# A hybrid decoder step on one core: state sums one unit sooner, two output strips interleaved, and a new order of the last steps

## The chip, the cores and the metric

One core of a Trainium2 chip runs one launch of the kernel. The metric is the device time in microseconds (us), as the median of the runs.

## The reference

One step of a hybrid decoder layer, for a prompt of 256 tokens (with 16 learned meta tokens ahead of it) and for 8 samples of one token. D is 2048, there are 8 heads with DK = 128 and DV = 256, and the feed-forward width is 5632.

```python
h = rmsnorm(x, norm1_g)
z = h @ w_in                              # u, cg, bg, q, k, v, o, gates, g_a, g_b
a_out = bg * causal_dwconv(cg * u)
hb    = mlstm_sequence(q, k, v, ...)      # per head: C = carry * C + sum g k v^T
mix   = sigmoid(g_a) * a_out + sigmoid(g_b) * sigmoid(o) * hb
x     = x + mix @ w_out
up    = causal_dwconv(rmsnorm(x, norm2_g) @ w_up)
x     = x + (silu(up[..., D_FF:]) * up[..., :D_FF]) @ w_down
y     = rmsnorm(x, norm_f_g)              # written for the prompt and the samples
```

The matrix memories C, the normalisers n and m, and the rows of both convolutions are outputs as well. All tensors are float32.

## The kernel before

Everything lives on one core, with the 280 tokens along the free dimension and features along the partitions. All four large products use the same **unit**: 8 tiles of 128 by 128 of the weight matrix (1024 columns of a slot), one column block of 128 outputs. Each unit passes four engines in turn. SP loads it into `w_raw` (512 KB), ScalarE (ACT) copies it into `w_hi`, which rounds it to the type fp32r, VectorE (DVE) writes the rest into `w_lo = w_raw - w_hi`, and TensorE (PE) multiplies: per tile `w_hi` with the high and the low part of the activations (16 matmuls, L1324), then `w_lo` with the high part (8 matmuls, L1329). There are 4 slots (`RING`), so the semaphores let ACT write `w_hi` of unit u+4 only when PE has used unit u (`unit_used`), and let SP load again into a slot when DVE has written its `w_lo` (`lo_done`). Two units make a **strip**, whose sum gathers in one PSUM bank (strip0 to strip3 in turn) and is then taken out by DVE. `evacuated` counts strips taken out, and the second half of a strip waits for the bank of the next one.

The program has these stages, each engine with its own list of instructions written out by hand:

- The start: loads, transposes of x, the first norm (`rtok`, spread over partitions as `rbc`) and the gates.
- Eight heads. Each has 16 strips of `w_in`, which are units 0 to 31 of the head. Functions `front` (units 0 to 7) and `back` (units 8 to 31) of each engine hold the order: the loop variable `i` is the unit's number in the head, `step(n, HEAD_U, 0, i)` splits the unit that is 4 later (i + 4), and the work of the head is inserted between the steps. In `back`, GpSimd (POOL) updates the sample states `c_st` in four pairs (L564, L565, L569, semaphore `c_updated`). DVE sums each pair with the query into `sacc` (L1056, L1060), in the steps i = 16, 17, 18 and 19, adds both halves (L1065) in i = 19, and PE multiplies them with `sel` (L1436) after strip 10, which is unit 21. That is the **state sum**. In the same steps DVE takes out the strips `ga` (i = 15), `go` (17) and `gb` (19) on L889, and ACT has its sigmoids of them in the same list as the copies to `w_hi`.
- The output projection: 16 strips of `w_out`, the activations are `mh` and `ml`, in 16 tiles. The last tile comes from the last head: POOL makes `mx`, DVE splits it into `mh` and `ml` (L1097, L1100, semaphore `mix_split`, 2 for each tile). Then a norm over the new x (`refine` on `rbc`).
- The feed-forward part in two halves: strips of `w_up`, the gated unit, strips of `w_down` (3 units each).
- The end: in the last 16 down strips, DVE adds x (L1199) and scales by the gain (L1204), PE transposes the result back to tokens (`turn_y`, L1227), ACT squares (L786) and POOL adds the squares into `acc` (L612). After the last strip PE sums `acc` over partitions (L1528, one column for each token tile), DVE, ACT and DVE again make 1/sqrt of the mean (L1208, L858, `refine`), and the rows are scaled: ACT the second 128 tokens in four column blocks, each followed by its own store (L866, L868), DVE the first 128 tokens in four blocks and the samples (L1218, L1220, L1221), which SP stores (L423, L425).

`refine` is a Newton step for 1/sqrt and is called three times: at the start on 128x3, after the output projection on 128x266, and at the end on 128x3. Two places carry the order of the state sum and of the end:

```python
if 16 <= i < 20:                                   # DVE, back(n)
    jp = i - 16
    v.wait_ge(c_updated, n * (JG // 2) + (jp + 1))
...
turn_y(KT - 1)                                     # PE, the end
pe.wait_ge(acc_done, 2 * KT + 1)
```

## Time and profile before

| what | value |
|---|---|
| median of 3 runs | 1744.8 us |
| lowest and highest | 1744.09 and 1752.38 us |
| the profiled execution, its own time | 1743.8 us |
| its span, first to last instruction | 1742.0 us |
| granted TensorE clock, mean | 0.997 |
| PE busy | 1721.4 us (99%) |
| DVE, ACT, POOL busy | 1157.7, 743.4, 482.7 us |

Busy time of PE is modelled: the matmuls overlap, and the end of each is an estimate, so its stalls are best read from the starts of two successive instructions. The time of the execution is 1.8 us above the span.

### The profile page before, as it was taken

What the parts mean: (1) busy time and instruction counts of PE and PEld (TensorE: products, weight loads), DVE (VectorE), ACT (ScalarE), POOL (GpSimd) and SP (SyncE); (2) the same over time, 40 slices, a digit from 0 to 9 for tenths busy, and PEclk for the clock granted to TensorE, in tenths of its full rate; (3) what the DMA queues carried; (4) which work ended last, traced back from release to release, by engine and by line L of the source; (5) the groups of instructions that cost most, each with busy time, mean ns of one, the idle gap of its engine ahead of it and who ended that gap; (6) DMA issues with size and microseconds to landing.
All of it is one profiled execution on the core that took longest, in us unless ns stands there. A gap on an engine that the chain in (4) does not pass through costs nothing.

```text
span 1742.0 us, 37212 instructions
## 1 busy us (share of the span) xinstructions
PE 1721.4 (99%) x13797; PEld 1706.3 (98%) x13797; DVE 1157.7 (66%) x1776; ACT 743.4 (43%) x867; POOL 482.7 (28%) x474
## 2 busy tenths in 40 slices
PE   9999999999999999999999999999999999999997
PEld 7999999999999999999999999999999999999997
DVE  4774757657485765748677887777555777777553
ACT  6534334344433433443345554554343333334443
POOL 3541615234161523416211222222000222222000
PEclk9999999999999999999999999999999999999998
DMA  7878685777868678786665666666666666666663
GB/s 192 205 198 194 181 212 149 214 189 203 199 176 206 159 212 186 201 207 172 183 172 159 188 186 174 179 177 176 183 179 186 171 180 180 176 179 181 172 178 105
DMA packets 591287, 318.78 MB, mean 183 GB/s; under 512 B 16695, under 2 KB 585847, under 8 KB 589103
## 3 DMA queue, kind: packets, MB, share of 16 engines
q1 hardware_dynamic: 578855, 293.13, 62.5%
q10 hardware_dynamic: 11944, 22.14, 4.6%
q0 software_dynamic: 400, 2.20, 0.5%
q8 instruction: 72, 1.18, 0.3%
q14 instruction: 16, 0.13, 0.0%
HBM read 305.07 MB, written 12.78 MB: 182 GB/s over the span
## 4 chain that ended last, share of the span: by engine, by line
PE 91%; DVE 5%; issue 3%; ACT 1%; DMA 0%; POOL 0%; DVEq 0%; ACTq 0%; SPq 0%; POOLq 0%
PE strip L1324 57%; PE strip L1329 29%; DVE w_lo L880 2%; PE aux L1227 1%; DVE sacc L1060 1%; PE aux L1420 1%; PE aux L1424 1%; DVE rden L1041 1%; DVE sacc L1056 0%; ACT w_hi L620 0%; PE aux L1393 0%; PE aux L1277 0%; PE strip L1260 0%; DMA x_tok<-in_x_prompt 0%; PE aux L1436 0%
## 5 line engine op out<-in xcount | busy, mean ns | idle before, releaser
L880 DVE TENSOR_TENSOR w_lo<-w_raw,w_hi 128x1024 fp32r<-128x1024 f32 x556 | 718.2, 1294 | 380.0 <-ACT w_hi L620 377.7
L620 ACT ACTIVATE w_hi<-w_raw 128x1024 fp32r<-128x1024 f32 x560 | 593.4, 1060 | 869.0 <-PE strip L1329 841.0
L1324 PE MATMUL strip<-xh,w_hi 128*128 128x266 f32 (+2 forms) x3424 | 866.4, 287 | 0.0
L1324 PE MATMUL strip<-xl,w_hi 128*128 128x266 f32 (+2 forms) x3424 | 864.5, 286 | 0.0
L1324 PEld LDWEIGHTS strip<-xh,w_hi 128*128 128x128 f32 x3424 | 644.8, 188 | 0.3
L1324 PEld LDWEIGHTS strip<-xl,w_hi 128*128 128x128 f32 x3424 | 644.1, 188 | 0.0
L1329 PE MATMUL strip<-xh,w_lo 128*128 128x266 f32 (+2 forms) x3424 | 494.1, 286 | 0.0
L1329 PEld LDWEIGHTS strip<-xh,w_lo 128*128 128x128 f32 x3424 | 451.4, 188 | 0.0
L1324 PE MATMUL strip<-hh,w_hi 128*128 128x264 f32 x704 | 176.2, 286 | 0.0
L1324 PE MATMUL strip<-hl,w_hi 128*128 128x264 f32 x704 | 174.7, 283 | 0.0
L604 POOL TENSOR_TENSOR gg<-sg,cz 128x264 f32<-128x264 f32 x44 | 58.2, 1322 | 412.1 <-ACT sg L825 412.1
L1324 PEld LDWEIGHTS strip<-hh,w_hi 128*128 128x128 f32 x704 | 132.4, 188 | 0.3
L1324 PEld LDWEIGHTS strip<-hl,w_hi 128*128 128x128 f32 x704 | 132.3, 188 | 0.0
L607 POOL TENSOR_TENSOR hid<-gg,cz 128x264 f32<-128x264 f32 x44 | 73.5, 1671 | 104.7 <-DVE cz L1168 104.7
L1329 PE MATMUL strip<-hh,w_lo 128*128 128x264 f32 x704 | 100.6, 283 | 0.0
L1329 PEld LDWEIGHTS strip<-hh,w_lo 128*128 128x128 f32 x704 | 91.5, 188 | 0.0
L1324 PE MATMUL strip<-mh,w_hi 128*128 128x266 f32 x256 | 64.5, 286 | 0.9 <-DVE ml L1100 0.9
L1324 PE MATMUL strip<-ml,w_hi 128*128 128x266 f32 x256 | 64.4, 286 | 0.0
L889 DVE TENSOR_TENSOR zs<-strip,rbc 128x266 f32<-128x266 f32 x88 | 37.9, 431 | 25.2 <-PE strip L1329 25.2
L578 POOL TENSOR_TENSOR so<-so,sbm 128x266 f32<-128x266 f32 x16 | 20.6, 1287 | 117.3 <-ACT sbm L765 117.3
L1160 DVE SCALAR_TENSOR_TENSOR cz<-zs,vecs,cz 128x256 f32<-128x256 f32 x88 | 42.7, 485 | 12.9 <-DVE cz L1157 2.1
L569 POOL TENSOR_TENSOR c_st<-c_st,kv 128x512 f32<-128x512 f32 x32 | 50.4, 1575 | 2.5
(284 smaller groups left out, 1262.5 us busy)
## 6 DMA issues: line engine op xcount, KB each, us to landing
w_raw<-in_w_in SPq DMA_DIRECT2D x256, 512.0 KB, 4.3
w_raw<-in_w_up SPq DMA_DIRECT2D x176, 512.0 KB, 4.1
w_raw<-in_w_down SPq DMA_DIRECT2D x64, 512.0 KB, 3.9
w_raw<-in_w_out SPq DMA_DIRECT2D x32, 512.0 KB, 4.0
w_raw<-in_w_down SPq DMA_DIRECT2D x32, 384.0 KB, 3.3
out<-c_st ACTq DMA_DIRECT2D x8, 1024.0 KB, 7.1
c_st<-in_state_mlstm_C ACTq DMA_DIRECT2D x7, 1024.0 KB, 11.2
rb<-scratch_rows ACTq DMA_DIRECT2D x8, 270.0 KB, 4.6
```

What stands on the lines that cost most here:

```text
L569: g.tensor_tensor(c_p, c_p, kv[:, :, :], ALU.add).then_inc(c_updated, 1)
L578: g.tensor_tensor(so[:, :], so[:, :], sbm[:, :], ALU.mult).then_inc(p_gate, 1)
L604: g.tensor_tensor(gg[:, :], sg[:, :], cz[:, 0, :], ALU.mult).then_inc(gg_done, 1)
L607: g.tensor_tensor(hid[:, :], gg[:, :], cz[:, 1, :], ALU.mult).then_inc(hid_done, 1)
L620: act.activation(w_hi[:, slot, :], w_raw[:, slot, :], ACT.Copy).then_inc(hi_done, 1)
L880: v.tensor_tensor(w_lo[:, slot, :], w_raw[:, slot, :], w_hi[:, slot, :].bitcast(f32), ALU.subtract).then_inc(lo_done, 1)
L889: v.tensor_tensor(out, bank[b][:, 0:width], rbc[:, c0:c0 + width], ALU.mult).then_inc(evacuated, 1)
L1041: v.reciprocal(rden[:, :], den[:, :])\
L1060: v.scalar_tensor_tensor(out=sacc[:, a, :], in0=c_st[:, jg, :], scalar=qkd_g[:, jg:jg + 1], in1=sacc[:, a, :], op0=ALU.mult, op1=ALU.add). ...
L1160: v.scalar_tensor_tensor(out=cz[:, z, 0:SEQ], in0=zs[:, z, 1:1 + SEQ], scalar=wcol[1], in1=cz[:, z, 0:SEQ], op0=ALU.mult, op1=ALU.add)\
L1324: pe.matmul(bank[b][:, 0:c1 - c0], w_hi[:, slot, w], xt[:, k0 + k, c0:c1], start=(first and k == 0 and t == 0), stop=False)
L1329: mm = pe.matmul(bank[b][:, 0:c1 - c0], w_lo[:, slot, w], rh[:, k0 + k, c0:c1], start=False, stop=(last and k == kk - 1))
```

## The change

Four edits:

- **State sums.** DVE does the four pairs in steps i = 15 to 18 instead of 16 to 19, and the final addition in step 18. The operations are the same.
- **First two output strips.** PE's order was first half and second half of strip 0, then of strip 1. It is now first half of strip 0, first half of strip 1, second half of strip 0, second half of strip 1. The first half of strip 1 does not count as a used unit when it ends (`frees=0`); the second half of strip 0 counts for both.
- **`refine`.** Its last two operations, an addition of 1.5 and a multiplication, become one.
- **The end.** POOL no longer adds the last square. PE sums `acc` with the first 15 squares and then the last square `sqs` itself, into one column each of three PSUM banks, ahead of the last `turn_y`. DVE has three operations for the mean instead of two. Of ACT's four blocks the third (columns 1024 to 1535) goes to DVE and its store to SP. Only the last blocks still wait for the last `turn_y`.

```diff
@@ -417,11 +417,11 @@

-            for h in range(4):
+            for i, (t, h) in enumerate(((0, 0), (0, 1), (0, 2), (1, 2), (0, 3))):
                 c = slice(h * D // 4, (h + 1) * D // 4)
-                sp.wait_ge(y_done, h + 1)
-                sp.dma_start(y_prompt[0, 0:P, c], yt[:, 0, c]).then_inc(stored, 16)
-            sp.wait_ge(y_done, 5)
+                sp.wait_ge(y_done, i + 1)
+                sp.dma_start(y_prompt[0, t * P:(t + 1) * P, c], yt[:, t, c]).then_inc(stored, 16)
+            sp.wait_ge(y_done, 6)
             sp.dma_start(y_sample[:, 0, :], ys[:, :]).then_inc(stored, 16)
@@ -606,7 +606,7 @@
             g.wait_ge(acc_clear, 1)
-            with g.Fori(KT, 2 * KT) as m:
+            with g.Fori(KT, 2 * KT - 1) as m:
                 g.wait_ge(sq_done, m + 2)
@@ -854,17 +854,18 @@
                     act.activation(ys[:, 512 * gq:512 * gq + 512], aux[2][0:NS, :], ACT.Copy).then_inc(y_copied, 1)
-            act.wait_ge(rf_step, 2)
+            act.wait_ge(rf_step, 3)
             act.activation(rfr[:, :], rfm[:, :], ACT.Sqrt).then_inc(rf_root, 1)
...
             act.wait_ge(y_copied, 3 * (KT // 4 - 1))
-            act.wait_ge(y_turned, KT)
-            for h in range(4):
+            for i, h in enumerate((0, 1, 3)):
                 c = slice(h * D // 4, (h + 1) * D // 4)
+                if h == 3:
+                    act.wait_ge(y_turned, KT)
                 src = yt[:, 1, c] if h < 3 else aux[1][:, :]
                 act.activation(yt[:, 1, c], src, ACT.Copy, scale=rf[:, 1:2]).then_inc(y1_done, 1)
-                act.wait_ge(y1_done, h + 1)
+                act.wait_ge(y1_done, i + 1)
                 act.dma_start(y_prompt[0, P:2 * P, c], yt[:, 1, c]).then_inc(stored, 16)
@@ -897,9 +898,8 @@
                 v.wait_ge(done, d0 + 3)
-                v.tensor_scalar(root[0:r, c], root[0:r, c], 1.5, None, ALU.add).then_inc(done, 1)
-                v.wait_ge(done, d0 + 4)
-                v.tensor_tensor(out[0:r, c], out[0:r, c], root[0:r, c], ALU.mult).then_inc(done, 1)
+                v.scalar_tensor_tensor(out=out[0:r, c], in0=root[0:r, c], scalar=1.5, in1=out[0:r, c],
+                                       op0=ALU.add, op1=ALU.mult).then_inc(done, 1)

@@ -928,7 +928,7 @@
             refine(P, slice(0, 3), rms, msq, rtok, rtok_done, 0)
-            v.wait_ge(rtok_done, 5)
+            v.wait_ge(rtok_done, 4)
             for j in range(3):
@@ -1045,9 +1045,9 @@
                          .then_inc(h_step, 1)
-                    if 16 <= i < 20:
-
-                        jp = i - 16
+                    if 15 <= i < 19:
+
+                        jp = i - 15
                         sa0 = n * (JG + 1)
@@ -1060,7 +1060,7 @@
                                                        op0=ALU.mult, op1=ALU.add).then_inc(sacc_step, 1)
-                        if i == 19:
+                        if i == 18:
                             v.wait_ge(sacc_step, sa0 + JG)
@@ -1136,7 +1136,7 @@
             refine(P, slice(0, NM), rt2, rm2, rbc, r2_step, 1)
-            v.wait_ge(r2_step, 6)
+            v.wait_ge(r2_step, 5)

@@ -1205,20 +1205,21 @@
             v.wait_ge(acc_clear, 2)
-            v.tensor_scalar(rfm[:, 0:2], aux[3][:, 0:2], 1.0 / D, EPS, ALU.mult, ALU.add).then_inc(rf_step, 1)
-            v.tensor_scalar(rfm[0:NS, 2:3], aux[3][0:NS, 2:3], 1.0 / D, EPS, ALU.mult, ALU.add).then_inc(rf_step, 1)
+            for j, b in enumerate((aux[3], bank[0], bank[1])):
+                r = P if j < 2 else NS
+                v.tensor_scalar(rfm[0:r, j:j + 1], b[0:r, 0:1], 1.0 / D, EPS, ALU.mult, ALU.add).then_inc(rf_step, 1)
             v.wait_ge(rf_root, 1)
-            refine(P, slice(0, 3), rfr, rfm, rf, rf_step, 2)
+            refine(P, slice(0, 3), rfr, rfm, rf, rf_step, 3)
             v.wait_ge(rf_step, 7)
             v.wait_ge(y_copied, 3 * (KT // 4 - 1))
+            q = D // 4
+            for t, h in ((0, 0), (0, 1), (0, 2), (1, 2)):
+                c = slice(h * q, (h + 1) * q)
+                v.tensor_scalar(yt[:, t, c], yt[:, t, c], rf[:, t:t + 1], None, ALU.mult).then_inc(y_done, 1)
             v.wait_ge(y_turned, KT)
-            for h in range(4):
-                c = slice(h * D // 4, (h + 1) * D // 4)
-                src = yt[:, 0, c] if h < 3 else aux[0][:, :]
-                v.tensor_scalar(yt[:, 0, c], src, rf[:, 0:1], None, ALU.mult).then_inc(y_done, 1)
-            c = 3 * D // 4
-            v.tensor_scalar(ys[:, 0:c], ys[:, 0:c], rf[0:NS, 2:3], None, ALU.mult)
-            v.tensor_scalar(ys[:, c:D], aux[2][0:NS, :], rf[0:NS, 2:3], None, ALU.mult).then_inc(y_done, 1)
+            v.tensor_scalar(yt[:, 0, 3 * q:D], aux[0][:, :], rf[:, 0:1], None, ALU.mult).then_inc(y_done, 1)
+            v.tensor_scalar(ys[:, 0:3 * q], ys[:, 0:3 * q], rf[0:NS, 2:3], None, ALU.mult)
+            v.tensor_scalar(ys[:, 3 * q:D], aux[2][0:NS, :], rf[0:NS, 2:3], None, ALU.mult).then_inc(y_done, 1)

@@ -1311,7 +1312,7 @@

-            def unit(u, slot, b, k0, kk, rh, rl, c0, c1, first, last, waits=()):
+            def unit(u, slot, b, k0, kk, rh, rl, c0, c1, first, last, waits=(), frees=1):

@@ -1328,7 +1329,8 @@
                                    start=False, stop=(last and k == kk - 1))
-                mm.then_inc(unit_used, 1)
+                if frees:
+                    mm.then_inc(unit_used, frees)

@@ -1448,8 +1450,14 @@

-            out_strip(0, 0, tiles_ready(mix_split, 2, 0, KT))
-            for q in range(1, 4):
+            def out_unit(q, h, waits, frees):
+                unit(U_B + 2 * q + h, 2 * q + h, q, h * KU, KU, mh, ml, 0, NM, h == 0, h == 1, waits, frees)
+
+            out_unit(0, 0, ((0, mix_split, KT),), 1)
+            out_unit(1, 0, ((0, evacuated, S_B + 2),), 0)
+            out_unit(0, 1, ((0, mix_split, 2 * (KT - 2)), (KU - 2, mix_split, 2 * (KT - 1)), (KU - 1, mix_split, 2 * KT)), 2)
+            out_unit(1, 1, ((2, evacuated, S_B + 3),), 1)
+            for q in range(2, 4):
                 out_strip(0, q)
@@ -1521,12 +1529,18 @@
                     turn_y(m - 1)
+
+            def sums(squares, first, last):
+                for j, b in enumerate((aux[3], bank[0], bank[1])):
+                    r = P if j < 2 else NS
+                    mm = pe.matmul(b[0:r, 0:1], squares[:, j * P:j * P + r], ones[:, 0:1], start=first, stop=last)
+                return mm
+
+            pe.wait_ge(acc_done, 2 * KT)
+            sums(acc, True, False)
+            pe.wait_ge(sq_done, 2 * KT + 1)
+            sums(sqs, False, True).then_inc(ssqf_done, 1)
             turn_y(KT - 1)
-            pe.wait_ge(acc_done, 2 * KT + 1)
-            for j in range(3):
-                r = P if j < 2 else NS
-                mm = pe.matmul(aux[3][0:r, j:j + 1], acc[:, j * P:j * P + r], ones[:, 0:1], start=True, stop=True)
-            mm.then_inc(ssqf_done, 1)

```

VectorE in the last head, around the state sum (`sacc`). `w_lo` is the low part of a weight unit, `gb` a strip taken out, `pn_new` a normaliser column. Before:

```order
L880 TENSOR_TENSOR w_lo<-w_raw,w_hi 128x1024 [waits hi_done]
L1060 SCALAR_TENSOR_TENSOR sacc<-c_st,qkd_g,sacc 128x256 [waits sacc_step,c_updated]
L1060 SCALAR_TENSOR_TENSOR sacc<-c_st,qkd_g,sacc 128x256 [waits sacc_step]
L1069 TENSOR_SCALAR pn_new<-pc 128x1 [waits pc_done]
L889 TENSOR_TENSOR gb<-strip,rbc 128x266 [waits unit_used]
L880 TENSOR_TENSOR w_lo<-w_raw,w_hi 128x1024 [waits hi_done]
L1060 SCALAR_TENSOR_TENSOR sacc<-c_st,qkd_g,sacc 128x256 [waits sacc_step,c_updated]
L1060 SCALAR_TENSOR_TENSOR sacc<-c_st,qkd_g,sacc 128x256 [waits sacc_step]
L1065 TENSOR_TENSOR sacc<-sacc 128x256 [waits sacc_step]
L880 TENSOR_TENSOR w_lo<-w_raw,w_hi 128x1024 [waits hi_done]
```

And of the changed kernel:

```order
L881 TENSOR_TENSOR w_lo<-w_raw,w_hi 128x1024 [waits hi_done]
L1060 SCALAR_TENSOR_TENSOR sacc<-c_st,qkd_g,sacc 128x256 [waits sacc_step,c_updated]
L1060 SCALAR_TENSOR_TENSOR sacc<-c_st,qkd_g,sacc 128x256 [waits sacc_step]
L1065 TENSOR_TENSOR sacc<-sacc 128x256 [waits sacc_step]
L1069 TENSOR_SCALAR pn_new<-pc 128x1 [waits pc_done]
L890 TENSOR_TENSOR gb<-strip,rbc 128x266 [waits unit_used]
L881 TENSOR_TENSOR w_lo<-w_raw,w_hi 128x1024 [waits hi_done] x2
```

The last addition (L1065) now stands ahead of `pn_new`, `gb` and one `w_lo`, and `gb` and that `w_lo` behind all the sums.

TensorE at the end of the first unit of the output projection. strip0 and strip1 are PSUM banks, `mh_49` and `ml_50` the high and low part of the activations. Before:

```order
L1329 MATMUL strip0<-mh_49,w_lo 128x266 [waits lo_done]
L1329 MATMUL strip0<-mh_49,w_lo 128x266 x7
L1324 MATMUL strip0<-mh_49,w_hi 128x266 [waits mix_split,hi_done]
L1324 MATMUL strip0<-ml_50,w_hi 128x266
L1324 MATMUL strip0<-mh_49,w_hi 128x266
```

And of the changed kernel:

```order
L1330 MATMUL strip0<-mh_49,w_lo 128x266 [waits lo_done]
L1330 MATMUL strip0<-mh_49,w_lo 128x266 x7
L1325 MATMUL strip1<-mh_49,w_hi 128x266 [waits evacuated,hi_done]
L1325 MATMUL strip1<-ml_50,w_hi 128x266
L1325 MATMUL strip1<-mh_49,w_hi 128x266
```

The unit that follows no longer needs `mix_split`, the tiles of the last head, but the third weight unit of the projection and a free second bank.

TensorE's last instructions. L1227 (L1228) transposes `xg3_137`, the output before its scaling; aux0 to aux3 are PSUM banks. Before:

```order
L1227 MATMUL aux0<-ident,xg3_137 128x128 [waits x3_step]
L1227 MATMUL aux1<-ident,xg3_137 128x128
L1227 MATMUL aux2<-ident,xg3_137 8x128
L1528 MATMUL aux3<-ones,acc 128x1 [waits acc_done]
L1528 MATMUL aux3<-ones,acc 128x1
L1528 MATMUL aux3<-ones,acc 8x1
```

And of the changed kernel:

```order
L1536 MATMUL aux3<-ones,acc 128x1 [waits acc_done]
L1536 MATMUL strip0<-ones,acc 128x1
L1536 MATMUL strip1<-ones,acc 8x1
L1536 MATMUL aux3<-ones,sqs_125 128x1 [waits sq_done]
L1536 MATMUL strip0<-ones,sqs_125 128x1
L1536 MATMUL strip1<-ones,sqs_125 8x1
L1228 MATMUL aux0<-ident,xg3_137 128x128 [waits x3_step]
L1228 MATMUL aux1<-ident,xg3_137 128x128
L1228 MATMUL aux2<-ident,xg3_137 8x128
```

The sums stand ahead of the last transposes, and there are six in place of three.

## Rows read from the trace of the kernel before

**Rows 1.** The page: the chain that ended last, shares of the span by engine.

```profile
PE 91%; DVE 5%; issue 3%; ACT 1%; DMA 0%; POOL 0%; DVEq 0%; ACTq 0%; SPq 0%; POOLq 0%
```

**Rows 2.** L1436 in the view by line: idle time before it, us, times.

```profile
  issue: 5.0, 7
  DVE sacc L1065: 3.6, 6
```

**Rows 3.** Timeline, PE around L1436 in heads 0, 2 and 7: start, us, instruction.

```profile
101.82 1.14 PE L1329 MATMUL strip<-xh,w_lo 128*128 128x268 f32 x8
105.24 0.58 PE L1436 MATMUL aux<-sel,sacc 128*128 128x8 f32 x4 [2.27 <-DVE sacc L1065]
...
307.70 1.14 PE L1329 MATMUL strip<-xh,w_lo 128*128 128x268 f32 x8
309.06 0.58 PE L1436 MATMUL aux<-sel,sacc 128*128 128x8 f32 x4 [0.21 <-DVE sacc L1065]
...
817.56 1.14 PE L1329 MATMUL strip<-xh,w_lo 128*128 128x268 f32 x8
818.59 0.58 PE L1436 MATMUL aux<-sel,sacc 128*128 128x8 f32 x4
```

**Rows 4.** Timeline, DVE in head 0, steps 17 to 19.

```profile
95.26 1.71 DVE L880 TENSOR_TENSOR w_lo<-w_raw,w_hi 128x1024 fp32r<-128x1024 f32 x1
96.89 2.42 DVE L1060 SCALAR_TENSOR_TENSOR sacc<-c_st,qkd_g,sacc 128x256 f32<-128x256 f32 x2
99.23 1.77 DVE L880 TENSOR_TENSOR w_lo<-w_raw,w_hi 128x1024 fp32r<-128x1024 f32 x1
...
101.72 0.14 DVE L1069 TENSOR_SCALAR pn_new<-pc 128x1 f32 x1
...
102.13 1.21 DVE L880 TENSOR_TENSOR w_lo<-w_raw,w_hi 128x1024 fp32r<-128x1024 f32 x1
103.27 1.36 DVE L1060 SCALAR_TENSOR_TENSOR sacc<-c_st,qkd_g,sacc 128x256 f32<-128x256 f32 x2
104.66 0.42 DVE L1065 TENSOR_TENSOR sacc<-sacc 128x256 f32<-128x256 f32 x1
```

**Rows 5.** Timeline, POOL in head 0: the last update of the states.

```profile
95.97 2.15 POOL L569 TENSOR_TENSOR c_st<-c_st,kv 128x512 f32<-128x512 f32 x1
```

**Rows 6.** Timeline, first strip of the output projection: DVE's third unit, and PE.

```profile
847.18 1.23 DVE L880 TENSOR_TENSOR w_lo<-w_raw,w_hi 128x1024 fp32r<-128x1024 f32 x1 [1.74 <-ACT w_hi L620]
...
853.34 0.28 PE L1324 MATMUL strip<-ml,w_hi 128*128 128x266 f32 x1
854.49 0.39 PE L1324 MATMUL strip<-mh,w_hi 128*128 128x266 f32 x1 [0.86 <-DVE ml L1100]
```

**Rows 7.** Timeline, the end: last square, sums, root, scaling, ACT's last store.

```profile
1729.19 1.28 ACT L858 ACT_TABLE_LOAD   x1
1729.33 0.74 POOL L612 TENSOR_TENSOR acc<-acc,sqs 128x264 f32<-128x264 f32 x1 [7.43 <-ACT sqs L786]
1730.12 0.73 PE L1528 MATMUL aux<-ones,acc 128*128 128x1 f32 x6 [0.41 <-POOL acc L612]
...
1731.13 0.21 ACT L858 ACTIVATE rfs<-rfs 128x3 f32<-128x3 f32 x1 [0.67 <-DVE rfs L1209]
...
1731.98 0.17 DVE L900 TENSOR_SCALAR rfs<-rfs 128x3 f32<-128x3 f32 x1
...
1732.38 0.72 ACT L866 ACTIVATE yt<-yt,rfs 128x512 f32<-128x512 f32 x1 [1.04 <-DVE rfs L902]
...
1735.92 0.53 SPq L425 DMA_DIRECT2D out<-ys  x1
1736.59 0.34 ACTq L868 DMA_DIRECT2D out<-yt  x1
```

**Rows 8.** Windows of the end: us, busy us of the engines, PEclk, DMA share, GB/s.

```profile
1736.00:1737.00 1.00, 0.00 (x0) 0.00 (x0) 0.00 (x0) 0.56 (x1) 0.00 (x0) 0.50 1.07 246
1737.00:1738.00 1.00, 0.00 (x0) 0.00 (x0) 0.00 (x0) 0.00 (x0) 0.00 (x0) 0.50 1.05 395
```

## The prediction

> **What bounds the kernel now.** I read the page first, then PE's waits, then PE's timeline round each, and last the end. The chain by engine [rows 1] is PE for 91% of the span: a microsecond counts only if PE stands still in it, or if it lies behind PE's last matmul. DVE's 5% of the chain belongs to stretches in which DVE's list is late and PE waits at their end. That is the state sum. PE stands before L1436 in seven heads, 5.0 us in all on the side of the weight loads, and 3.6 us over six waits on the matmul side [rows 2]; the matmul side is too low, because the modelled end of the matmuls before covers a part. So I take starts [rows 3]. In head 7 L1436 starts 1.03 us after the group of eight L1329, and no wait is named: that is the undisturbed distance. In head 0 it is 3.42 us, in head 2 it is 1.36 us, so PE lost 2.39 us in the first and 0.33 us in the other. Heads 1 and 3 to 6 look like head 2.
>
> There is one more stall of a microsecond: in the second half of the first output strip PE stops between two successive matmuls, 853.34 and 854.49 us, on the last tile of `ml` [rows 6]. The pitch of these matmuls is about 0.12 us, so 1.03 us are lost. Behind PE there is the end: last square, POOL's addition, the sum on PE, root, scaling, stores [rows 7]. From ACT's table load at 1729.19 us, which follows the last square at once, to the end of the span at 1742.0 us are 12.8 us. Everything else that the change touches has no stall of PE beside it.
>
> **State sums.** No operation is added or removed, the order alone changes. The last addition (L1065) is pulled ahead of `pn_new`, the take-out of `gb` and one `w_lo`. Before, `pn_new` started at 101.72 us and the sums of the last pair at 103.27 us [rows 4], so these three took 1.55 us, and the addition ends 1.55 us sooner. For that to be right DVE must have no idle time in between, and its rows follow each other without any. In head 0 this cuts PE's stall from 2.39 to about 0.84 us; in the six heads with 0.33 us it goes altogether, with 1.2 us to spare. Gain: 1.55 + 6 x 0.33 = **3.5 us**. The bounds: below, only the 3.6 us of the matmul side with head 0 counted as 2.27 and cut by 1.55 give 1.55 + 1.33 = 2.9 us; above, the 5.0 us less the rest in head 0 give 4.2 us.
>
> What is now late instead? In the steps 15 to 17 each `w_lo` stands behind one more pair. In head 0 the low part of unit 21 began at 95.26 us and took 1.71 us; with the pair at 96.89 us, which lasts until 99.23 us, ahead of it, it would be ready about 2.3 us later, at 99.3 us [rows 4]. PE uses it at 101.82 us [rows 3]: 2.5 us are left, the smallest margin that I find. The loads that SP may start after a `w_lo`, and ACT's next copy behind the sigmoids of `go` and `gb`, slip with it by the same amount at most, and PE reaches them three units later, some 9 us. The new wait on POOL is no wait: the last update of the states in head 0 ends at 98.12 us [rows 5], and its sums come after about 101.5 us in the new order.
>
> A look at contention: beside POOL's updates a `w_lo` takes 1.71 and 1.77 us, and 1.21 us when POOL is done [rows 4]. The sums of the third pair now run nearer to POOL's work, but the same list of DVE work stands beside the same POOL work, so I take nothing for it; a further blocked operation would add about 0.5 us in head 0, once. By the Trainium skill (page "SBUF — State Buffer", section on the two separate sides) DVE operations with two SBUF inputs and GpSimd operations hold a shared pair of ports exclusively, and the loser waits for the whole instruction, which speaks against moving sums toward POOL's stretch. By that rule one more loser waits up to a whole POOL operation, and the gain in head 0 would be about 0.5 instead of 1.55 us.
>
> **First output strips.** The second unit no longer needs the last tile. It takes the third weight unit instead, whose low part DVE began at 847.18 us and had in 1.23 us [rows 6], over 3 us before PE wants it. The tile is then wanted about 3 us later than now, and the stall of 1.03 us becomes none. Gain **1.0 us**. The price: slots of the second and third unit come free together, one unit later for the former. ACT and DVE have then two units to split in a row, about 1.2 us each on DVE, and PE needs the first of them two units (6 us) later. I cost it at nothing; the cover is the ring of 4 slots.
>
> **`refine`.** One operation less in each of the three calls. The first call ends before PE spreads its result between two halves of a strip, the second is hidden by PE's first up strips, where no stall stands. Both gain nothing; the third is on the path, below.
>
> **The end.** PE now waits for the square only. Before, the sums started at 1730.12 us; now the six matmuls on `acc` run while ACT squares, and those on the square can begin when ACT is done, at about 1729.19 us, when its table load starts [rows 7]. Six matmul instructions take the same 0.73 us, so DVE has the sums about 0.9 us sooner, and pays about 0.07 us for the third operation (my estimate: it overlaps most of the one before it). But the root can't start before the table load ends, 1729.19 + 1.28 = 1730.47 us. It started at 1731.13 us, so only 0.64 us of some 0.85 us arrive [rows 7]. `refine` gives 0.2 us more (L900 alone takes 0.17 us). All scaling starts 0.84 us sooner, at 1731.54 us.
>
> From there ACT has three blocks instead of four. Its first block began at 1732.38 us and its fourth store was issued at 1736.59 us; less the 0.72 us of a block, that is three times 1.16 us [rows 7]. Its last store would be issued at 1736.59 - 0.84 - 1.16 = 1734.6 us. DVE has one block more (0.4 us), so SP's store of the samples comes at 1735.92 - 0.84 + 0.4 = 1735.5 us, now the last one issued, 1.1 us ahead of the last one of before. Does the end follow? The stores move 2.16 MB (264 rows of 8 KB). The windows show the DMA share at its full value from 1736 us on, first 246 and then 395 GB/s [rows 8]: it is the transfers that drain, not the issue. So the lower value is the sooner start, 0.84 us, and the upper one the 1.1 us; one could lose 0.4 us of it if SP's queue, with 5 blocks and the samples, drains alone at the lower rate. I take **1.0 us**, between 0.4 and 1.5. By the Trainium skill (page "DMA: Bandwidth & Descriptors", section "Issuing engines are not separate DMA queues") it makes no difference for the drain which engine issues a transfer. The spread of 246 to 395 GB/s in the same mix of stores neither proves nor refutes it; by that rule the gain would be the 0.84 us of the sooner start alone.
>
> **Sum.** 3.5 + 1.0 + 1.0 = 5.5 us less. The profiled execution took 1743.8 us, which gives 1738.3 us for such an execution. The median of the three runs is 1.0 us above it, and I forecast that: 1744.8 - 5.5 = **1739.3 us**. It is 0.3%, and below the 0.5% (8.7 us) that a measurement of this kernel can tell from no change: the three runs alone span 8 us. From the ends of the terms (2.9 + 0.5 + 0.4 = 3.8 and 4.2 + 1.1 + 1.5 = 6.8 us) this case reaches from 1738.0 to 1741.0 us.
>
> **The rivals.** First, the stalls are not removed but moved (10%): PE gets to the next place at which it must wait for weights 0.33 us sooner, and gives it back there. For it speaks that DVE, ACT and SP feed PE at its own pace; against it, that DVE is idle for 1.74 us before it splits a unit of the projection [rows 6], thus is ahead there, and no other wait of PE has this form. Only the end and part of head 0 would stay: 1.0 + 1.0 = 2.0 us, 1742.8 us.
>
> Second, slower (3%): the pulled-forward sums make a `w_lo` late. The place is the low part of unit 21 (and 20) of each head, the price what exceeds the margin of 2.5 us. If the pairs met POOL's updates fully, as in head 0 where a pair lasted until 2.3 us later, plus another such one in each head, PE would wait 1 to 2 us per head; with 8 heads and 1.5 us that is 12 us more, against 5.5 us gained: 1744.8 + 12 - 2 = 1754.8 us. It decides from 3 us per DVE pair on. Against it: outside head 0 POOL is done with the states earlier in relation to DVE, and DVE's total in these steps stays.
>
> Third, more than the sum (5%): freeing head 0 and the other heads lets the whole ring run ahead, and the small excesses of the first matmul after each L1436 go as well, with some other stalls hidden by modelled ends. With twice the 4.5 us of the heads and the projection the gain would be 10 us, 1734.8 us.
>
> Fourth, the part of the sums goes as forecast but the output strips do not gain (7%): ACT's bunched copies stall PE by the same 1 us two units on. Then 1740.3 us.
>
> **How the numbers follow.** The forecast 75%, the rivals 10, 3, 5 and 7%. The level of the runs moves as well: the lowest of before is 0.7 us under its median and one lies 7.6 us over it. The range takes the forecast's own 1738.0 to 1741.0 us, the first rival at 1742.8 us and this spread: 1736.0 to 1743.8 us. Faster by over 0.5% needs a time under 1736.1 us: the third rival and a low level of the runs, 7%. Slower by over 0.5% is the second rival, 3%. The rest, 90%, is within 0.5%.
>
> **What would show it.** In the changed profile: L1436 starts 1.03 us after its L1329 in seven heads, and 1.9 us in head 0; L1065 ends before `gb` is taken out; no idle time of PE on `ml`; the sums on the square start at about 1729.2 us on the old scale and the root right at the end of the table load, so that table load becomes what releases it; SP's store of the samples is the last issue. Wrong would be: PE waits for `w_lo` or `w_hi` in the steps 20 to 23 of a head, L1436 in head 0 still over 2 us late, or a last transfer that ends no sooner after the last L1199 than before.

## The result and the profile after

The changed kernel takes 1736.7 us (median of 6 runs, 1736.37 to 1738.25), the kernel before 1744.63 us (6 runs). The ratio of the runs is 0.9945, 95% interval 0.9933 to 0.9956: 0.55% less, or 7.9 us between the medians, where 5.5 us were forecast. The profiled executions took 1743.8 and 1736.41 us, with spans of 1742.0 and 1734.7 us, so 7.3 us of span. The forecast, 1739.3 us, is 2.6 us too high: the time lies in the stated range (1736.0 to 1743.8 us), but below the forecast's own 1738.0 to 1741.0 us, and the change is just over the 0.5% that I had called out of reach.

The waits of PE in the changed kernel, microseconds in total, times, longest. The waits for the state sum and for `ml` are gone [rows 2, 6]; POOL's addition at the end is replaced by a wait of 0.2 us for the square:

```profile
PE aux L1236 <- POOL a L438: 2.1, 1, 2.1
PE strip L1271 <- DVE w_lo L922: 0.6, 1, 0.6
PE strip L1228 <- DMA x_tok<-in_x_prompt: 0.5, 1, 0.5
PE strip L1261 <- DVE xl L916: 0.4, 1, 0.4
PE aux L1536 <- ACT sqs L786: 0.2, 1, 0.2
```

The chain by engine: PE went from 91% [rows 1] to 98%, since the stretches of DVE's list that led to the state sums left it:

```profile
PE 98%; DVE 1%; DMA 0%; ACT 0%; issue 0%; SPq 0%; DVEq 0%
```

The timeline of PE round the state sum (L1438 now) in heads 0, 2 and 7, against [rows 3]:

```profile
101.81 1.14 PE L1330 MATMUL strip<-xh,w_lo 128*128 128x268 f32 x8
102.99 0.58 PE L1438 MATMUL aux<-sel,sacc 128*128 128x8 f32 x4
...
305.20 1.15 PE L1330 MATMUL strip<-xh,w_lo 128*128 128x268 f32 x8
306.19 0.51 PE L1438 MATMUL aux<-sel,sacc 128*128 128x8 f32 x4
...
812.94 1.15 PE L1330 MATMUL strip<-xh,w_lo 128*128 128x268 f32 x8
813.92 0.51 PE L1438 MATMUL aux<-sel,sacc 128*128 128x8 f32 x4
```

The distance is 1.18 us in head 0 and 0.98 to 0.99 us in the others. So the undisturbed distance is 0.98 us; the 1.03 us of head 7 that I had read as such held a small wait.

All 560 groups of eight L1329 (L1330) stand in both traces, and the difference of their starts tells where the time went. It moves by more than 0.04 us in ten places only:

| place | shift of the first unit behind it, us | forecast, us |
|---|---|---|
| after the state sum of head 0 | -2.24 | -1.55 |
| heads 1 to 6 | -0.36, -0.43, -0.44, -0.65, -0.45, -0.44 | six times -0.33 |
| head 7 | -0.13 | 0 |
| second unit of the output projection | -1.11 | -1.03 |
| last L1199 to the end of the span | -1.45 | -1.0 |
| sum, less 0.4 us given back | -7.3 | -5.5 |

Behind the state sums of heads 0 to 6 the next two units give back 0.06 us each time, 0.4 us in all. So the heads keep 4.75 us (2.19 us in head 0, 2.56 us in the seven others), and with 1.11 and 1.45 us these are the 7.3 us.

VectorE in head 0 of the changed kernel, against [rows 4]:

```profile
96.68 1.97 DVE L881 TENSOR_TENSOR w_lo<-w_raw,w_hi 128x1024 fp32r<-128x1024 f32 x1
98.56 1.89 DVE L1060 SCALAR_TENSOR_TENSOR sacc<-c_st,qkd_g,sacc 128x256 f32<-128x256 f32 x2
100.38 1.21 DVE L881 TENSOR_TENSOR w_lo<-w_raw,w_hi 128x1024 fp32r<-128x1024 f32 x1
101.51 0.87 DVE L1060 SCALAR_TENSOR_TENSOR sacc<-c_st,qkd_g,sacc 128x256 f32<-128x256 f32 x2
102.42 0.42 DVE L1065 TENSOR_TENSOR sacc<-sacc 128x256 f32<-128x256 f32 x1
```

The last pair takes 0.87 us, where it took 1.36 us. The low part of unit 21 is there at 98.65 us and used at 101.81 us, 3.2 us later; I had left it 2.5 us.

The end of the changed kernel, against [rows 7]:

```profile
1722.43 0.43 DVE L1199 TENSOR_TENSOR x<-strip,xres 128x264 f32<-128x264 f32 x1 [7.36 <-PE strip L1330]
...
1723.34 1.28 ACT L858 ACT_TABLE_LOAD   x1
...
1724.63 0.21 ACT L858 ACTIVATE rfs<-rfs 128x3 f32<-128x3 f32 x1
...
1725.67 0.72 ACT L867 ACTIVATE yt<-yt,rfs 128x512 f32<-128x512 f32 x1 [0.83 <-DVE rfs L901]
...
1728.73 0.34 ACTq L869 DMA_DIRECT2D out<-yt  x1
1728.85 0.73 DVE L1222 TENSOR_SCALAR ys<-aux,rfs 8x512 f32<-8x512 f32 x1
1729.91 1.19 SPq L425 DMA_DIRECT2D out<-ys  x1
```

The root (L858) starts right at the end of the table load, as forecast. From the last L1199 the scaling begins after 3.24 us (before 4.10), and the span ends 9.03 us after that (before 9.62). Spans are read to 0.1 us here and below, so such a stretch can be off by 0.05 us.

### The profile page after: what moved, and what is told of

It is laid out like the page before. It is cut to its first block, busy times and chain, and to the rows that moved or that the text cites. A ratio compares the mean times of both kernels' runs of the same rounds, so it can differ in the third digit from the quotient of the medians.

```text
span 1734.7 us, 37218 instructions
## 1 busy us (share of the span) xinstructions
PE 1720.7 (99%) x13803; PEld 1707.1 (98%) x13803; DVE 1155.1 (67%) x1775; ACT 741.5 (43%) x866; POOL 480.5 (28%) x473
## 3 DMA queue, kind: packets, MB, share of 16 engines
q8 instruction: 72, 1.18, 0.3%
## 4 chain that ended last, share of the span: by engine, by line
PE 98%; DVE 1%; DMA 0%; ACT 0%; issue 0%; SPq 0%; DVEq 0%
PE strip L1325 62%; PE strip L1330 31%; PE aux L1228 1%; PE aux L1422 1%; PE aux L1426 1%; PE aux L1395 0%; PE aux L1278 0%; PE strip L1261 0%; DMA x_tok<-in_x_prompt 0%; PE aux L1236 0%; PE strip L1271 0%; PE aux L1438 0%; DVE xl L916 0%; PE strip L1228 0%; ACT xh L637 0%
## 5 line engine op out<-in xcount | busy, mean ns | idle before, releaser
L1330 PE MATMUL strip<-xh,w_lo 128*128 128x266 f32 (+2 forms) x3424 | 494.4, 286 | 0.0
L1330 PEld LDWEIGHTS strip<-xh,w_lo 128*128 128x128 f32 x3424 | 451.6, 188 | 0.0
L1330 PE MATMUL strip<-hh,w_lo 128*128 128x264 f32 x704 | 100.6, 283 | 0.0
L1330 PEld LDWEIGHTS strip<-hh,w_lo 128*128 128x128 f32 x704 | 91.5, 188 | 0.0
L578 POOL TENSOR_TENSOR so<-so,sbm 128x266 f32<-128x266 f32 x16 | 20.6, 1285 | 129.1 <-ACT sbm L765 129.1
L564 POOL TENSOR_TENSOR c_st<-c_st,qkd_g 128x512 f32<-128x512 f32 x32 | 46.7, 1459 | 6.5 <-DMA vg<-scratch_v 4.6
```

The source lines that it names most:

```text
L564: g.tensor_tensor(c_p, c_p, dec_p, ALU.mult).then_inc(dec_done, 1)
L578: g.tensor_tensor(so[:, :], so[:, :], sbm[:, :], ALU.mult).then_inc(p_gate, 1)
L1330: mm = pe.matmul(bank[b][:, 0:c1 - c0], w_lo[:, slot, w], rh[:, k0 + k, c0:c1], start=False, stop=(last and k == kk - 1))
```

## The experiments

Five kernels (e1 to e5) carry one part of the change each, the others test a cause. Each was timed beside the kernel before on the same chip. The kernel before is 1745.8 to 1747.2 us there, with single runs from 1743.4 to 1752.6 us; why it spreads more than the changed kernel is a question of its own, taken up with e14.

**e1, the state sums alone.**

```diff
-                    if 16 <= i < 20:
+                    if 15 <= i < 19:
-                        jp = i - 16
+                        jp = i - 15
...
-                        if i == 19:
+                        if i == 18:
```

> The kernel before with the state sums one unit sooner, and nothing else. Theory (each edit acts in its own stage and they add up): the state sums alone bring 4.7 to 4.8 us, of them 2.25 us in head 0 and about 0.36 us in each of heads 1 to 7, as the shift of PE's units between the two traces says; time about 1739.9 us against 1744.6. Rival (edits lean on each other, so that a part of the 7.3 us of span exists only with all of them): under 4 us here, and the four single edits do not sum to the whole.

Measured: 1740.54 us against 1746.16 us, ratio 0.9969 (0.9955 to 0.9983). In the trace heads 1 to 7 give -0.36, -0.44, -0.44, -0.64, -0.46, -0.44 and -0.12 us, as in the changed kernel to 0.01 us. Head 0 gave 1.58 us in this execution, with a distance of 1.84 us to L1436. The theory of edits that add up holds for heads 1 to 7; head 0 differs between executions. The traces show where. POOL's first state update of head 0 ends 1.0 us before DVE starts the list of this stretch (L1034, 85.05 us) in the kernel before, and 1.2 us after that start (86.13 us) in e1. Before, and then e1:

```profile
82.75 1.29 POOL L569 TENSOR_TENSOR c_st<-c_st,kv 128x512 f32<-128x512 f32 x1
...
85.12 2.24 POOL L569 TENSOR_TENSOR c_st<-c_st,kv 128x512 f32<-128x512 f32 x1
```

With POOL's updates late, DVE needs 18.93 us from L1034 (start) to the end of L1065, and 17.89 us in the changed kernel's profile, where POOL is as early as before. The old order has both cases too: 20.03 us with POOL early, 21.15 us with POOL late (e5). So the new order shortens this stretch by 2.1 to 2.2 us in either case, and a late POOL costs about 1.1 us of it. What makes POOL late in some executions stays open.

**e6, only the last pair ahead.**

```diff
-                    if 16 <= i < 20:
-                        jp = i - 16
+                    for jp in ({16: (0,), 17: (1,), 18: (2, 3)}.get(i, ())):
...
-                        if i == 19:
+                        if jp == 3:
```

> The kernel before, but only the last pair of sums and the final addition are pulled ahead of pn_new, gb and one w_lo; the first three pairs stay in their old steps. Theory (contention): of head 0's 2.25 us the reordering of the last pair is 1.55 us, and the rest is VectorE time lost to GpSimd's state updates that the earlier first pairs avoid; so PE's distance from L1329 to L1436 in head 0 falls from 3.42 to about 1.85 us here, against 1.18 us with all pairs moved, and the time is about 0.7 us above that of the sums alone. Rival (the position of the first three pairs does not matter, and the 1.55 us were merely misread): head 0's distance falls to 1.2 us here as well, same time as the sums alone.

Measured: 1739.62 us (1738.98 to 1741.22), ratio 0.9963 (0.9952 to 0.9975), no slower than e1; distance 1.55 us, shift in head 0 -1.87 us. My theory was that the earlier first pairs avoid state updates. DVE's time from L1034 (start) to the end of L1065 in head 0 does not depend on when the stretch begins, and POOL is early in all three of these: 20.03 us before, 18.00 us here, 17.89 us in the changed kernel. So the last pair alone brings 2.03 us and the three others 0.11 us. The theory falls, and so does the rival, whose 1.2 us of distance did not come. The rows say what I had overlooked:

```profile
99.70 1.78 DVE L880 TENSOR_TENSOR w_lo<-w_raw,w_hi 128x1024 fp32r<-128x1024 f32 x1
101.41 1.66 DVE L1059 SCALAR_TENSOR_TENSOR sacc<-c_st,qkd_g,sacc 128x256 f32<-128x256 f32 x4
103.10 0.42 DVE L1064 TENSOR_TENSOR sacc<-sacc 128x256 f32<-128x256 f32 x1
103.44 0.15 DVE L1068 TENSOR_SCALAR pn_new<-pc 128x1 f32 x1
103.51 0.42 DVE L889 TENSOR_TENSOR gb<-strip,rbc 128x266 f32<-128x266 f32 x1
```

and POOL, in the kernel before and then in e6:

```profile
102.81 1.14 POOL L578 TENSOR_TENSOR so<-so,sbm 128x266 f32<-128x266 f32 x1 [2.89 <-ACT sbm L765]
...
104.53 1.17 POOL L578 TENSOR_TENSOR so<-so,sbm 128x266 f32<-128x266 f32 x1 [4.13 <-ACT sbm L765]
```

Two pairs take 1.66 us, 0.8 us each. In the old order the last pair (1.36 us, [rows 4]) stood behind the take-out of `gb`. That take-out lets ACT make its sigmoid, and the sigmoid lets POOL multiply the gates (L578): before, from 102.81 to 103.95 us, while the pair begins at 103.27 us. In every head of the kernel before the last pair takes 1.36 to 1.39 us, and 0.87 us in every head of e6. The pair now runs before DVE has released that work, and POOL starts it after the pair. 1.55 us of order and 0.5 us of this make the 2.03 us.

**e8 and e9, the state updates made small.** GpSimd's three operations of each update act on 2x8 of 2x256 columns; the rest of the states is not updated. e9 has the sums of e1 as well.

```diff
-  g.tensor_tensor(c_p, c_p, dec_p, ALU.mult)
+  g.tensor_tensor(c_p[:, :, 0:8], c_p[:, :, 0:8], dec_p[:, :, 0:8], ALU.mult)
```

(and in the same way for `kv` and the addition)

> The kernel before, with GpSimd's three operations of each state update on 2x8 of 2x256 columns, so that the states are not updated in the rest. It takes GpSimd's long operations away from beside VectorE. Theory (contention): VectorE's low parts take 1.2 us throughout the steps 14 to 19, the pairs 0.9 us (the first 0.8 to 0.9), and PE's distance to L1436 in head 0 falls from 3.42 to the undisturbed 1.0 us, since 3 to 4 us of lost VectorE time are gone. Rival (VectorE is late in head 0 for another reason, such as the split of a late weight unit): the distance stays over 2 us.

> The same with the sums one unit sooner. Theory: nothing is left for the reordering to gain, PE's units run as in the other small variant within 0.1 us per head. Rival: the reordering still gains 1.5 us in head 0.

Measured, one run each: 1738.89 and 1738.96 us, distances 0.99 and 0.98 us. PE's units run together to 0.2 us, so nothing is left for the reordering: the theory holds in both, but for one pair of e8. DVE in e8:

```profile
93.64 0.88 DVE L1060 SCALAR_TENSOR_TENSOR sacc<-c_st,qkd_g,sacc 128x256 f32<-128x256 f32 x2
...
96.61 0.87 DVE L1060 SCALAR_TENSOR_TENSOR sacc<-c_st,qkd_g,sacc 128x256 f32<-128x256 f32 x2
...
99.56 1.38 DVE L1060 SCALAR_TENSOR_TENSOR sacc<-c_st,qkd_g,sacc 128x256 f32<-128x256 f32 x2
```

and POOL's gate product in e8:

```profile
98.85 1.42 POOL L578 TENSOR_TENSOR so<-so,sbm 128x266 f32<-128x266 f32 x1 [8.45 <-ACT sbm L765]
```

The second pair is down from 2.42 to 0.9 us and the third is at 0.87 us as before, but the last one still takes 1.38 us with the updates all but gone. What blocks it is not the state update; it is the gate product that runs from 98.85 to 100.27 us. In e9, where the last pair stands ahead of it, the pair takes 0.87 us. No run takes the gate product itself out. DVE's stretch is 16.65 us in e8 instead of 20.03 us: the state updates cost DVE 3.4 us in head 0, and without them there is no stall there.

**e2, the output strips alone** (the edits of `out_unit` and `frees` in the diff above).

> The kernel before with the first two output strips half by half, and nothing else. Theory: PE's stall of 1.03 us on ml goes, no new one comes; 1.0 to 1.1 us less, time about 1743.5 us. Rival (the bunched slots stall PE later): no gain, 1744.6 us, with a gap of PE before the fifth or sixth unit of the projection.

Measured: 1743.59 us, ratio 0.9982 (0.997 to 0.9993). The shift at the second unit of the projection is -1.11 us, and nothing is given back behind it. The theory holds, and the rival with the bunched slots falls.

**e3, the new sums at the end alone** (PE's `sums`, the three operations for the mean).

> The kernel before with the last square summed on PE ahead of the last turn, three operations for the mean, but the old refine and the old division of the scaling. Theory: the root starts at the end of ACT's table load, 0.64 us sooner, and everything behind shifts by it: the stretch from the last L1199 to the end of the span falls from 13.72 to about 13.1 us. Rival (the end is set by transfers that do not care when they are issued): under 0.3 us.

Measured: 1746.48 us against 1746.16 us, ratio 1.0004 (0.9989 to 1.0019), which does not resolve it. In the trace the root comes 2.20 us after the last L1199 (before 2.85) and the span ends 13.12 us after it (before 13.72): 0.60 us. The theory holds.

**e5, `refine` alone.**

> The kernel before with the merged last step of refine alone, in all three calls. Theory: 0.2 us at the end and nothing in the first two calls, so 1744.4 us, which the timing hardly resolves; in the trace the stretch from the root to the first scaling falls from 1.25 to 1.05 us, and the shift of PE's units stays zero after both other calls.

Measured: 1745.9 us, ratio 0.9999 (0.999 to 1.0009). From the root to the scaling 1.04 us (before 1.25), and no shift of PE's units behind either of the other calls: 0.21 us, as expected.

**e4 and e7, the block (1,2).** e4 is the kernel before with the new division of the scaling alone; e7 is the changed kernel with the old one.

> The kernel before with the block (1,2) scaled by VectorE and stored by SP, ACT three blocks, and nothing else. All scaling starts when it did. Theory A (the stores drain as a sum of bytes): no sooner start, so no gain, under 0.2 us. Theory B (before, ACT's queue ends alone and slowly because its last store is issued last; the move lets both queues end together): 0.5 to 0.7 us less from the first scaling to the end of the span (9.62 before, 9.0 here). Theory C (the last issue sets the end): 1.1 minus 0.4, thus about 0.3 us, since the samples' store moves back by 0.4 us and is at 1736.3 on the old scale.

> The changed kernel with the old division of the scaling. Theory B: the stretch from the first scaling to the end of the span is 9.6 us as before, 0.5 to 0.6 us longer than with the move, time about 1737.3 us against 1736.7. Theory A: same time as the changed kernel. The start of the scaling behind the last L1199 is 3.24 us in either case.

Measured: e4 1747.17 us against 1747.07 us (0.9982 to 1.001), e7 1739.66 us. First scaling to the end of the span: 9.01 us in e4, 9.64 us in e7, where the two originals have 9.62 and 9.03. The move is worth 0.61 us, whoever starts when. The time of e7 itself is 2.4 us over the expected 1737.3 us. Its profile (1740.56 us) shows why in that execution: POOL's updates are late in head 0 (DVE's stretch is 19.85 us), L1436 stands 2.91 us behind its L1329, and the granted clock is 0.57 from 106 to 110 us, which costs 1.6 us more. This clock is the matter of e14. Theory A falls, and C too, since the last issue of e4 is the samples' store, 4.23 us behind the first scaling, as late as ACT's last one before (4.21).

**e10, all stores by SP** (ACT's three `dma_start` become SP's, each behind `y1_done`).

> The changed kernel with all nine stores of y issued by SP, in the order in which the blocks are ready; ACT only scales. If it makes no difference for the drain who issues (the rule of the Trainium skill on issuing engines), the end comes within 0.3 us of the changed kernel's, unless SP's issues, some 0.4 to 0.9 us each, fall behind. If one queue alone drains at 230 to 250 GB/s and two at 350 to 400, as windows of both traces suggest, 2.16 MB take 2 to 3 us longer: about 1739 us.

Measured: 1737.02 us (1736.81 to 1737.8), first scaling to the end 8.97 us. One queue drains as fast as two, so the imbalance of the queues (theory B) is not it either. Its windows (us, PE, PEld, DVE, ACT, POOL busy, PEclk, DMA share, GB/s):

```profile
1728.00:1729.00 1.00, 0.00 (x0) 0.00 (x0) 1.00 (x2) 0.04 (x1) 0.00 (x0) 0.50 1.05 375
1729.00:1730.00 1.00, 0.00 (x0) 0.00 (x0) 1.00 (x2) 0.00 (x0) 0.00 (x0) 0.50 1.11 246
1730.00:1731.00 1.00, 0.00 (x0) 0.00 (x0) 0.04 (x1) 0.00 (x0) 0.00 (x0) 0.50 1.06 281
1731.00:1732.00 1.00, 0.00 (x0) 0.00 (x0) 0.00 (x0) 0.00 (x0) 0.00 (x0) 0.50 1.05 379
1732.00:1733.00 1.00, 0.00 (x0) 0.00 (x0) 0.00 (x0) 0.00 (x0) 0.00 (x0) 0.50 1.04 402
1733.00:1734.00 1.00, 0.00 (x0) 0.00 (x0) 0.00 (x0) 0.00 (x0) 0.00 (x0) 0.50 1.03 299
```

A single queue shows both 246 and 402 GB/s at a full share, the same as two queues in [rows 8]. Here the trace agrees with the Trainium skill (page "DMA: Bandwidth & Descriptors", section "Issuing engines are not separate DMA queues"), which I had left undecided. The kernel before has one slow microsecond more. Its last two microseconds of transfers:

```profile
1739.00:1740.00 1.00, 0.00 (x0) 0.00 (x0) 0.00 (x0) 0.00 (x0) 0.00 (x0) 0.50 0.94 203
1740.00:1741.00 1.00, 0.00 (x0) 0.00 (x0) 0.00 (x0) 0.00 (x0) 0.00 (x0) 0.50 0.55 197
```

The changed kernel's have 408 and 402 GB/s, and then the rest:

```profile
1731.00:1732.00 1.00, 0.00 (x0) 0.00 (x0) 0.00 (x0) 0.00 (x0) 0.00 (x0) 0.50 1.06 408
1732.00:1733.00 1.00, 0.00 (x0) 0.00 (x0) 0.00 (x0) 0.00 (x0) 0.00 (x0) 0.50 1.27 402
1733.00:1734.00 1.00, 0.00 (x0) 0.00 (x0) 0.00 (x0) 0.00 (x0) 0.00 (x0) 0.50 0.30 92
```

From 1739 us on it moves 203 GB/s at a share of 0.94, so the queues are not empty, while the changed kernel moves 402 GB/s at about the same distance from its first scaling (6.3 to 7.3 us against 6.6 to 7.6 us). An obvious cause would be the last large block (256 KB): ACT issues it 4.2 us behind the first scaling with four blocks, 3.1 us with three. But e10 issues its last large block later still, 4.4 us behind the first scaling (1726.12 us), and ends as early as the changed kernel:

```profile
1730.49 0.65 SPq L424 DMA_DIRECT2D out<-yt  x1
```

So the time of that issue alone is not the cause either. That the 0.6 us come from moving the block is shown by e4 and e7; why the kernel before has the slow microsecond stays open.

**e12, the sums two units sooner** (steps 14 to 17 in the changed kernel).

> The changed kernel with the sums another unit sooner (steps 14 to 17). It tests the margin that I named as the point of the slower case: each low part stands behind one pair more, 2 us later again, and VectorE would wait for GpSimd's last update in head 0 (98 us). Theory: margin of 2.5 us is about used up; the remaining 0.2 us of head 0 go, but PE stands at the low part of unit 20 or 21 for up to 1 us in head 0 and not in the others; time within 0.5 us of the changed kernel. Rival (slack is larger than I read): 0.2 us faster and no stall anywhere.

Measured: 1736.45 us (1736.23 to 1737.92), distance 0.98 us in head 0, no wait of PE in any head. The rival holds for the stalls: the slack is larger than I read. That the kernel is also 0.2 us faster is seen in the trace alone; four runs can't tell it from the changed kernel. Unit 21's low part is ready at 101.04 us there and used at 102.02 us, so 1.0 us is left, and the point at which the slower case would begin was still not reached.

**e13, the last pair alone in the changed kernel** (the edit of e6).

> The changed kernel with the first three pairs back in their old steps; only the last pair and the final addition stay ahead. Theory (the gain is the last pair's: it comes before the take-out of gb and so also before the gate product that GpSimd starts after it, which blocked the pair by 0.5 us): same time as the changed kernel within 0.4 us, distance to L1436 in head 0 about 1.5 us and undisturbed in the other heads. Rival (the early pairs carry half of it): over 0.7 us slower.

Measured on one chip: 1738.07 us (1736.52 to 1741.26) against 1737.96 us for the changed kernel once more (c_after), thus no difference that can be told. DVE's stretch is 18.01 against 17.89 us. The distance in head 0 was 1.97 us, where 1.5 us were expected, and 1.11 us in c_after, since DVE began the stretch 0.8 us later in that execution. That the gain is the last pair's is borne out; the earlier three make head 0 less sensitive at most.

> The changed kernel once more, beside variants on the same chip and as their measure: 1736.4 to 1738.3 us as before, while the kernel before spreads from 1743.5 to over 1750 us.

Measured: 1736.54 to 1738.8 us (4 runs), while the kernel before took 1743.97 to 1752.57 us beside it.

**e14, head 0 alone.** What spreads the kernel before? In three of the profiles with the old order (e2, e4, e5), and in e7 with the new order and POOL late, the units behind L1436 of head 0 run slowly. e4, windows behind the stall:

```profile
104.00:106.00 2.00, 0.64 (x6) 0.42 (x4) 2.00 (x3) 2.00 (x3) 1.14 (x1) 1.00 0.94 243
106.00:110.00 4.00, 3.24 (x15) 3.27 (x16) 3.19 (x5) 0.09 (x1) 0.00 (x0) 0.58 0.74 177
110.00:114.00 4.00, 4.00 (x21) 4.00 (x21) 0.00 (x0) 0.59 (x1) 0.00 (x0) 0.57 0.80 223
```

The granted clock fell to 0.58 and 0.57 over these windows, a mix of the two levels 2.4 and 1.2 GHz, after 2.1 us in which PE waited for the state sum. The two units behind it start 2.9 us later for it. e2 has the same (0.59 and 0.55, 3.0 us), e5 and e7 a shorter one (0.57 from 106 to 110 us only); it costs each of them 1.6 us, on top of the wait itself. The length of the wait alone does not decide: e3 and the kernel before had 1.00 there after waits of 2.32 and 2.27 us, e2 had the slow clock after 2.31 us and e7 after 1.77 us.

```diff
...
+            back(0, i0=14)
+            front(1)
-            with v.Fori(0, H - 1) as n:
+            with v.Fori(1, H - 1) as n:
```

(`i0` is the step of the first pair, 16 where nothing is given)

> The kernel before, with the sums two units sooner in head 0 alone, so that PE's long stall in head 0 is gone (distance 1.0 us), and nothing else. Theory (that stall also lowers TensorE's granted clock to about 0.57 for some 4 us behind it in part of the executions, as seen in three of the profiles, at 2 to 3 us each): median 3 us or more under the kernel before, not the 2.4 us of one undisturbed execution, near 1742 us, and a spread of under 3 us in place of 9. Rival (the spread comes from somewhere else, the start above all): the spread stays, and the median falls by 2.4 us or less.

Measured: 1742.35 us (1741.09 to 1746.7, 10 runs) against 1747.15 us, ratio 0.9978 (0.9965 to 0.9992). The medians are 4.8 us apart, the lowest runs 2.9 us, where the stall itself is 2.4 us. The interval of the ratio reaches from 1.4 to 6.1 us, so the runs fit the theory but do not separate it from the 2.4 us of the stall alone. That the clock behind the stall adds to the price of the state sum in some executions rests on the traces of e2, e4, e5 and e7. The spread did not fall under 3 us but to 5.6 us: half of the runs lie within 0.5 us, the others up to 5 us above. One more source is at the start. In this profile the clock was 0.75 from 16 to 20 us and PE 1.8 us later by 25 us, which comes in kernels of both orders (0.72 in e1 and 0.75 in e11 with the new one, 0.75 in e2 with the old one). I don't know what decides it.

**e11 and e15, an early table load.** A root of three columns ahead of the last square makes ACT load its table while PE works; e15 adds the sums of e12.

```diff
+                if m == KT - 1:
+                    act.wait_ge(acc_clear, 2)
+                    act.activation(rfr[:, :], rfm[:, :], ACT.Sqrt)
```

> The changed kernel with a root on three columns of ones ahead of the last square, so that ACT's table load runs while PE is in the last strip. Theory (in the changed kernel the root waits 0.2 us for the table load and not for the sums): the root starts 0.2 us sooner and the end by 0.2 us; 1736.5 us. Rival (the loads alternate: Square needs another table back): the table is loaded twice and the end is 1 us later.

> The changed kernel with the sums two units sooner (steps 14 to 17) and ACT's root table loaded ahead of the last square. Theory: 0.2 us from head 0 and 0.2 us from the root, 0.4 us under the changed kernel, and the stretch from first scaling to the end is 9.0 us (the 9.8 us of the single look at the early table were chance). Rival: the early table lengthens that stretch by 0.8 us again, and the whole is 0.4 us slower.

Measured: the load is not repeated, and the root comes 2.02 instead of 2.20 us after the last L1199 in both. e11 took 1737.26 us with 9.79 us from the first scaling to the end, e15 1736.16 us with 8.99 us; so the long end of e11 does not come with the edit. The runs of e11 show no gain (1736.5 us were expected). e15 has the lowest runs: four of its six are 1735.91 to 1736.35 us, under the lowest run of the changed kernel (1736.37), but the two others are at 1741 us. Its gain over the changed kernel shows in the trace (0.2 us in head 0 and 0.2 us at the root), and the runs are too few to show it in the median.

## Why the prediction was too small

1. **Undisturbed distance of 1.03 us.** Mis-sized. It is 0.98 us, and the matmuls behind a wait start late as well, so the heads 1 to 7 kept 2.56 us where 6 x 0.33 = 1.98 us stood. I had taken the one head without a named wait as free of one, and head 4, at 1.55 us, as like head 2 at 1.36 us.
2. **1.55 us in head 0.** This is the step that failed. I moved the last pair by the start-to-start time of what it passes and left its own duration of 1.36 us as it was, though a pair at 100.93 us took 0.87 us. Where I looked for contention, I looked at POOL's state updates and took nothing for it. e6 and e8 show the 0.5 us: the pair ran beside a gate product that the same list had just released. DVE's stretch became 2.14 us shorter, and PE gained 2.24 us (2.19 us kept). That e1 gave 1.58 us in head 0, nearly the forecast, is a coincidence: its list was only 1.1 us shorter, with POOL late, and began 0.5 us sooner against PE.
3. **The stall's second price.** The forecast counted PE's waiting time. The traces of e2, e4, e5 and e7 show that PE's clock behind the stall adds 1.6 to 3.0 us in some executions; the profile of before was not one of them. This may be why the medians are 0.6 us further apart than the spans, but no trace shows it.
4. **The output strips** were right: 1.03 us forecast, 1.11 us measured in two traces, and the bunched slots cost nothing.
5. **The end up to the scaling** was right to 0.02 us: 0.84 us forecast, 0.86 us measured, 0.65 us of it from the sums (up to the table load) and 0.21 us from `refine`.
6. **The stores**, 0.2 us beyond that, were mis-sized: 0.6 us. I took the drain as bound by its bytes from 1736 us on, since the DMA share was full. But the same share carries very different rates, and the kernel before has a microsecond at 203 GB/s which the changed kernel (402 GB/s) and e10 do not have. Who issues, and how late the last large block is issued, do not explain it (e10); its cause stays open.
7. The term costed at nothing, the lateness of `w_lo`, cost nothing, also with one unit more (e12). The slower case and the case of stalls that move did not occur.

Together: 4.75 us for the heads where 3.5 stood, 1.1 for 1.0, 1.45 for 1.0. That carried the change just over the half per cent that I had put out of reach: the 7% for a gain over the half per cent were too few, mostly because the upper end of the heads (4.2 us) was taken from what the waits view names, and items 1 and 2 missed to the same side beyond it.

## What to carry to other kernels

When an operation is moved within an engine's list, cost it by its duration at the new place, not the old one: look what its neighbours release on an engine that slows it down. Read a stall from starts, against the smallest distance over all repetitions, and add the granted clock of the microseconds behind it in more than one execution. A full DMA share does not say how fast stores drain: compare GB/s in the last windows with the best ones. And before one execution is set against another, look whether the engine beside it stands where it stood: here POOL's start moved a 2.2 us gain to 1.6 us.

## What the runs showed of the hardware that was not expected

- A pair of 128x256 operations on VectorE takes 0.87 us alone, 1.36 to 1.39 us beside one 128x266 operation of GpSimd, and up to 2.69 us beside its 128x512 updates (e1); a `w_lo` takes 1.21 us alone and up to 2.30 us beside them (e12). That is dearer than the 0.5 us per blocked operation that I took.
- TensorE's granted clock was 0.55 to 0.59 over one or two windows of 4 us behind a wait of 1.77 us (e7), 2.12 us (e4), 2.31 us (e2) and 2.92 us (e5), and stayed at 1.00 behind waits of 2.27 us (before) and 2.32 us (e3).
- One DMA queue carried the same 2.16 MB of stores in the same time as two (8.97 us from the first scaling against 9.03 us), at 246 to 402 GB/s from one microsecond to the next.
